# A hybrid mLSTM and S5 layer on one core: other orders in the first feed-forward round, a transfer for one weight sum, and another closing normalization

## What is computed

```python
h = rmsnorm(x, g_mix); proj = h @ w_in + b_in          # mixers A (mLSTM) and B (S5)
...
x = x + mix                                            # mix: gated outputs @ w_out
hf = rmsnorm(x, g_ffn)                                 # D_FF = 2816 = 22 tiles of 128
x = x + (silu(hf @ w_ff1) * (hf @ w_ff3)) @ w_ff2
y = rmsnorm(x, g_final)                                # returned, with the mixers' states
```

## Time and profile before

| | |
|---|---|
| median of 3 runs | 924.69 us (924.21 to 926.32) |
| the profiled execution: device time | 924.23 us |
| its span in the trace | 922.5 us |
| PE busy | 899.5 us (98% of the span) |
| DVE busy | 679.7 us (74%) |
| ACT busy | 506.6 us (55%) |
| POOL busy | 264.5 us (29%) |

### The profile page before, as it was taken

The page is one execution under the profiler, slowest core; times in us unless marked ns, Lnnn a source line. Parts: engine busy times, 40 slices in busy tenths (PEclk is TensorE's granted clock), DMA queues, the critical chain, the costliest instruction groups (busy, mean ns, idle before and its releaser), DMA issues. The chain is left out here.

```text
span 922.5 us, 20670 instructions
## 1 busy us (share of the span) xinstructions
PE 899.5 (98%) x8538; PEld 866.3 (94%) x8538; DVE 679.7 (74%) x1115; ACT 506.6 (55%) x860; POOL 264.5 (29%) x420
## 2 busy tenths in 40 slices
PE   8999999999999999999999999899999999999987
PEld 4899998999899899999999999899999999999976
DVE  6869993694596476954334479999987899877977
ACT  5469628918845974823333345666534566435542
POOL 6788876722724013000000001112211111212110
PEclk9999999999999999999999999999999999999998
DMA  7523137253336226352323536588888678888742
GB/s 304 184 81 107 68 103 265 104 223 129 106 119 229 72 80 237 102 219 95 114 92 114 139 114 136 119 215 183 181 176 185 159 183 193 196 175 172 147 90 93
DMA packets 50676, 138.44 MB, mean 150 GB/s; under 512 B 4340, under 2 KB 10020, under 8 KB 48664
## 3 DMA queue, kind: packets, MB, share of 16 engines
q1 hardware_dynamic: 31744, 79.64, 26.4%
q0 software_dynamic: 16608, 50.08, 24.2%
q10 hardware_dynamic: 2232, 7.41, 2.3%
HBM read 123.74 MB, written 13.39 MB: 149 GB/s over the span
## 5 line engine op out<-in xcount | busy, mean ns | idle before, releaser
L562 ACT ACTIVATE w_high<-raw 128x1024 fp32r<-128x1024 f32 (+1 forms) x146 | 152.2, 1047 | 171.5 <-PE G L1964 95.8
L1266 POOL DMA_DIRECT2D w_sums<-wst x34 | 48.4, 1423 | 413.5 <-DVE w_low L1769 284.8
L1304 DVE TENSOR_TENSOR w_low<-raw,w_high 128x1024 fp32r<-128x1024 f32 x78 | 98.0, 1263 | 80.5 <-ACT w_high L562 79.8
L1964 PE MATMUL G<-h_high,w_high 128*128 128x256 f32 (+1 forms) x640 | 130.9, 286 | 0.0
L1964 PE MATMUL G<-h_low,w_high 128*128 128x256 f32 (+1 forms) x640 | 129.0, 283 | 0.0
L1964 PE MATMUL G<-h_high,w_low 128*128 128x256 f32 (+1 forms) x640 | 128.9, 283 | 0.0
L1964 PEld LDWEIGHTS G<-h_high,w_high 128*128 128x128 f32 x640 | 99.2, 188 | 2.0 <-issue 1.6
L1964 PEld LDWEIGHTS G<-h_high,w_low 128*128 128x128 f32 x640 | 99.4, 188 | 0.0
L1964 PEld LDWEIGHTS G<-h_low,w_high 128*128 128x128 f32 x640 | 99.1, 188 | 0.0
L1769 DVE TENSOR_TENSOR w_low<-raw,w_high 128x1024 fp32r<-128x1024 f32 (+1 forms) x68 | 80.9, 1190 | 13.9 <-ACT w_high L562 13.7
L2286 PE MATMUL G<-ffn_in_high,w_high 128*128 128x260 f32 x308 | 87.3, 283 | 3.6 <-DVE up_a L1843 1.5
(11 more groups left out here) (455 smaller groups left out, 2422.5 us busy)
## 6 DMA issues: line engine op xcount, KB each, us to landing
raw<-wst SPq DMA_DIRECT2D x124, 512.0 KB, 3.5
w_sums<-wst POOLq DMA_DIRECT2D x30, 512.0 KB, 7.5
c_samples<-c POOLq DMA_DIRECT2D x4, 2048.0 KB, 8.8
out_cs<-c_samples POOLq DMA_DIRECT2D x4, 2048.0 KB, 7.6
w_sums<-wst SPq DMA_DIRECT2D x15, 512.0 KB, 4.5
raw<-wst POOLq DMA_DIRECT2D x15, 512.0 KB, 6.2
v_spread<-v_scratch ACTq DMA_DIRECT2D x4, 1024.0 KB, 6.3
raw<-wst SPq DMA_DIRECT2D x6, 384.0 KB, 3.2
```

Source lines behind the costliest of these rows:

```text
L562: return act.activation(out, in_, ACT.Copy, **kw)
L1266: pool.dma_start(halves_of(tile, r), block_of(r, row, col), accum_op=ALU.add).then_inc(s, 16)
L1304: tt(WL[n.slot()][:], raw[n.slot()][:], WH[n.slot()][:].bitcast(F32), ALU.subtract).then_inc(w_lo, 1)
L1964: last = mm(o, w[slot][:, c], h[:, k, c0_:c0_ + width], start=start and x == 0 and t == 0, stop=stop and x == n - 1 and t == 2)
```

## The change

`LAST` is 7, and `square_of(m)` holds the old wait and Square of chunk m. Two places are changed: the way from the last output chunk through the first up round, and the last two rounds with the end.

```diff
@@ SP @@
             for r in range(1, NR):
-                sp.wait_ge(s4_ready, r)
+                if r == 1:
+                    sp.wait_ge(s4_first, 16)
+                else:
+                    sp.wait_ge(s4_ready, r - 1)
                 load_a12(r)
...
@@ ACT @@
-                for q in ((0, 1), (2,), (3,))[m - 5] if m >= 5 else ():
+                for q in ((0, 1), (2,))[m - 5] if m in (5, 6) else ():
                     split_high(q)
+                if m < LAST:
+                    square_of(m)
+                else:
+                    act.activation(junk_a[:, 1:2], eps[:], ACT.Sqrt)
                 act.wait_ge(xg_ready, KC + m + 1)
...
+            split_high(3)
+            square_of(LAST)
@@ ACT, up_round @@
                 next_high(1)
                 next_high(2)
-                take(3, x, 0, took_x3)
                 if r == 0:
                     act.wait_ge(sq_summed, 2)
...
+                take(3, x, 0, took_x3)
                 next_high(3)
...
                 next_high(4)
+                if r == 0:
+                    act.activation(junk_a[:, 2:3], eps[:], ACT.Silu)
                 next_high(5)
@@ ACT, down_round @@
+                    if r == NR - 2 and i >= 5:
+                        for m in (0, 1) if i == 5 else (4, 5):
+                            act.wait_ge((took_z5, took_x6)[m // 4], 2 * r + m % 4 + 1)
+                            act.activation(sqf[m % 4 + m // 4 * 2][:], X1[:, m, :], ACT.Square).then_inc(sq_ready, 1)
+            def scale_by_gain(m, part):
+                copy(X1[:, m, part], X1[:, m, part], scale=g_fin[:, m:m + 1]).then_inc(gained, 1)
...
@@ POOL @@
                 sum_first(r)
+                if r == 0:
+                    pool.wait_ge(s_in[0], 32)
+                    pool.wait_ge(w_lo, N_FF + 4)
+                    pool.wait_ge(a12_in, 16)
+                    add_block(FB[0], 0, 0, 1, s4_first)
                 if r + 1 < NR:
                     sum_22(r + 1)
@@ DVE, output chunks @@
-                for q in ((0, 1), (2,), (3,))[m - 5] if m >= 5 else ():
+                for q in ((0, 1), (2,))[m - 5] if m in (5, 6) else ():
                     split_low(q)
-                if m == KC - 1:
-                    sum_12(0)
-                if m >= 1:
+                if 1 <= m < LAST:
                     add_square(m)
...
+            split_low(3)
+            add_square(LAST)
@@ DVE, down_round @@
-                        if last and i >= 5:
+                        if last and i == 6:
                             dve.wait_ge(s, 2 * r + su + 1)
-                            tt(sqh[2 * i - 6 + su][:], part, part, ALU.mult).then_inc(x2_late, 1)
+                            tt(sqh[6 + su][:], part, part, ALU.mult).then_inc(x2_late, 1)
                         if last and i == 6 and su == 0:
-                            invert(1)
+                            add_half_square(5, H1)
+                            add_half_square(6, H0)
+                    if last and i < 3:
+                        add_whole_square(i + 1)
+                    elif last and i < 5:
+                        for su in range(2):
+                            add_half_square(2 * i - 6 + su, (H0, H1)[i - 3])
+                    elif last and i == 5:
+                        add_half_square(4, H1)
                     for j in (i,) if then is None else then:
                         next_low(r, j)
...
-                    stt(part, part, g_fin[:, m:m + 1], (Q, G)[half][:, 3, 0:HALF], ALU.mult, ALU.mult).then_inc(y_dve, 1)
+                part = X1[:, m:m + 2, (H0, H1)[half]]
+                tt(part, part, (Q, G)[half][:, 3:4, 0:HALF].broadcast_to([P, 2, HALF]), ALU.mult).then_inc(y_dve, 1)
@@ PE @@
-                        elif r == NR - 1 and i == 6 and su == 1:
-                            part_product(r, i, su, ks[:1], True, False)
-                            sum_squares(1, range(3))
-                            sum_squares(0, range(1))
-                            last = part_product(r, i, su, ks[1:], False, True)
...
+            sum_squares(1, False)
+            sum_squares(0, False)
             spread_inverse(1)
-            sum_squares(0, range(1, 3))
+            sum_squares(0, True)
             spread_inverse(0)
```

More of the change, by code:

```diff
@@ L553, in _ @@
                 load_a22(r)
-            for half, m in [(half, m) for half in (1, 0) for m in range(0, KC, 2)]:
-                sp.wait_ge(y_dve, KC * (1 - half) + m + 1)
+            for count, (half, m) in enumerate(scale_order):
+                sp.wait_ge(y_dve, count + 1)
                 sp.dma_start(y_o[:, m, (H0, H1)[half]], X1[:, m, (H0, H1)[half]]).then_inc(y_out, 16)
@@ L585, in _ @@
             act.wait_ge(consts, 1)
-            act.activation(junk_a[:], eps[:], ACT.Sqrt)
+            act.activation(junk_a[:, 0:1], eps[:], ACT.Sqrt)
             act.wait_ge(w_in[0], 16)
@@ L991, in down_round, with final_part @@
+                    if r == NR - 1:
+                        final_part(r, i)
                 if r >= 2 and splits_late(r - 2):
                     hidden_high(up_index(r - 2), hid_at(r - 2))
+            def scale_by_gain(m, part):
+                copy(X1[:, m, part], X1[:, m, part], scale=g_fin[:, m:m + 1]).then_inc(gained, 1)
+            def final_part(r, i):
+                if i == 2 or i == 4:
+                    m0, part, s = (2, H0, took_y2) if i == 2 else (6, H1, took_x4)
+                    for su in range(2):
+                        act.wait_ge(s, 2 * r + su + 1)
+                        act.activation(sqh[i - 2 + su][:], X1[:, m0 + su, part], ACT.Square).then_inc(sq_ready, 1)
+                elif i == 3:
+                    act.wait_ge(sq_ready, 2 * KC + 4)
+                    for m in (0, 1, 4, 5):
+                        scale_by_gain(m, slice(0, T))
+                    act.wait_ge(sq_ready, 2 * KC + 6)
+                    for m in (2, 3):
+                        scale_by_gain(m, H0)
+                elif i == 5:
+                    for su in range(2):
+                        act.wait_ge(took_z5, 2 * r + su + 1)
+                        act.activation(sqh[4 + su][:], X1[:, 2 + su, H1], ACT.Square).then_inc(sq_ready, 1)
+                    act.wait_ge(sq_ready, 2 * KC + 8)
+                    for m in (6, 7):
+                        scale_by_gain(m, H1)
+                    act.activation(junk_a[:, 0:1], eps[:], ACT.Sqrt)
+                    act.wait_ge(sq_ready, 2 * KC + 10)
+                    for m in (2, 3):
+                        scale_by_gain(m, H1)
+                elif i == 6:
+                    for su in range(2):
+                        act.wait_ge(x2_late, su + 1)
+                        scale_by_gain(6 + su, H0)
+                        if su == 0:
+                            root_of_half(1)
@@ L994, in _, with root_of_half @@
+            def root_of_half(half):
+                act.wait_ge(sq_summed, 4 - half)
+                act.activation(rt[:, 3 * half:3 * half + 3], (Q, G)[half][:, 1, 0:3], ACT.Sqrt, bias=eps[:, 0:1], scale=1.0 / D).then_inc(root_ready, 1)
             for r, (kind, _, _) in enumerate(ROUNDS):
                 up_round(r) if kind == "up" else down_round(r)
[L996 to L998 removed]
```

119 lines of the change are left out of this document (55 added, 64 removed).

## The result

| | before | after |
|---|---|---|
| median of 6 runs each, taken together | 924.7 us (922.75 to 926.32) | 927.36 us (926.36 to 928.25) |
| ratio, with its 95% interval | 1 | 1.0032 (1.0017 to 1.0046) |
| the profiled execution: device time, span | 924.23, 922.5 us | 927.45, 925.7 us |
| PE, DVE, ACT busy | 899.5, 679.7, 506.6 us | 897.0, 677.6, 514.5 us |
| first product of round 0 to first of round 15 (the second last) | 561.68 to 872.26: 310.58 us | 561.28 to 874.46: 313.18 us |

The changed kernel is 0.3% slower, and the interval excludes no change. Of the 3.2 us between the two spans, 2.6 arise between the first product of round 0 and that of round 15. The end takes 1.0 us more, and the first product of round 0 came 0.4 earlier.

The account below looks back on a forecast made before the run. PE is busy for 98% of the span, so time is won or lost only at PE's stops and the end. 924.23 + 2.1 (first place) + 0.1 (end) = 926.4 us, range 923.4 to 928.0.

Parts of the forecast that it names:

- The stop in unit 2 goes: Round 0, last chunk's low part: PE's 1.15 us stop vanishes, about 1.3 us with the slow first matmul.
- Issue and landing: POOL's added transfer for unit 5's weights: issued at 569.85, takes 5.8 us, lands at 575.65.
- The reciprocal 1.4 later: DVE, ahead of round 1: the reciprocal starts at 579.7 in place of 578.28, +1.4 us.
- PE's stops: Round 0: PE stands 1.0 us at unit 5 and 3.2 us, not 1.5, ahead of round 1.
- The clock falls behind the stop: Behind the 3.2 us stop ahead of round 1: the clock likely falls, costing 1.7 us, partly covered by 0.95 us to spare.
- The first place +2.1: Last output chunk through first up round: +2.1 us with the clock's fall, +1.4 without.
- The last round: DVE's sums ahead of units 5 and 6's low parts delay unit 3's take; PE goes on 1.0 us later, stopping about 1.2.
- The end +0.1: Kernel's end: first scaling 0.6 us later, first output 0.85 later, denser output transfers save 0.7; together +0.1 us.
- The early landing: Rival: the added transfer lands as fast as a plain load, 3.5 us, giving 923.4; chance 0.12.
- The late one (7.3): Rival: the added transfer takes 7.3 us, everything behind it 1.5 later, giving 927.9; chance 0.18.
- The clock didn't hold: Concerns the rival that the clock holds behind the stop ahead of round 1, giving 925.7; chance 0.18.
- The end wasn't bound by DVE: Concerns the rival that DVE, not the transfers, bounds the end: 1.3 us less, giving 925.0; chance 0.12.

Follow-up runs that it names:

- The chunk's order alone: Kernel before with only the last chunk's high and low parts moved ahead; fourth sum on DVE, table loads, roots and end as before: 922.69 us, ratio 0.9987.
- the copies ahead: Changed kernel with ACT copying unit 3's product in round 0 ahead of unit 5's high part, so ahead of the wait for the transfer: 926.58 us, ratio 1.0038.
- the first place alone: Kernel before with the change from last chunk through first up round only, transfer included; last rounds and end as before: 926.87 us, ratio 1.0044.
- the sum on DVE: Changed kernel with round 0's fourth sum added by DVE, not the transfer: 921.33 us, ratio 0.9973; the same with before's end: 920.76 us, 0.9965.
- the kernel without early loads: Kernel before with the new first-up-round order, fourth sum on DVE, old end, but without the two early table loads (Sqrt, Silu): 921.57 us, ratio 0.9968.
- the end alone: Changed kernel with the first up round as before, so only the last two rounds and end changed: 924.35 us, ratio 1.0001.
- the sums behind: Changed kernel with round 0's fourth sum on DVE and, in the last round, DVE's three whole-square sums moved behind taking unit 3: 921.25 us, ratio 0.9970.
- the transfer alone: Kernel before with one edit: the first round's fourth sum made by POOL's adding transfer, not DVE; old order kept: 924.76 us, ratio 1.0003.

## Why the prediction was right, and where it wasn't

The forecast was 926.4 with a range to 928.0; 927.36 lies in it, and what came is "slower by over 0.2%", to which it gave 0.38 beside 0.52 for no change. The sum was made on the profiled execution: +2.2 there, where the two spans differ by 3.2 (2.6 for the first place, 1.0 for the end, less 0.4 for the earlier start). The mechanism (the transfer holds ACT, DVE and then PE, and the clock falls) is what the runs show. Its steps, in turn:

- **The stop in unit 2 goes: right.** The chunk's order alone brought 1.4 us (predicted 1.3).
- **Issue and landing: the issue right, the landing mis-sized.** Issued at 569.39 with a round that began 0.4 us earlier, that is at 569.8 on before's clock (predicted 569.85). It took 6.44 us, not 5.8, between the quiet row and the other. I called the stretch quiet, but another transfer of POOL, of which I knew, was under way with it. This trace has the longest of five: in the others ACT went on 5.99 to 6.25 us behind the issue, and 6.52 here, so 0.2 to 0.45 of the miss is there in all of them.
- **The reciprocal 1.4 later: right but for the landing.** It starts 18.67 us behind the first product of round 0, before 16.60: +2.07, which is the 1.4 and the 0.64 of the landing.
- **PE's stops: wrong place.** I had 1.0 us at unit 5 and 3.2 ahead of round 1. There was one of 5.22 at unit 4. The step that failed is my list of what is queued behind the wait: it named the high parts and roots and left out the copies of unit 3's product, which the change itself moved behind the roots. The order of ACT in the text ahead shows them. With the copies ahead of the wait, the trace had just the two stops of the prediction, 1.10 and 3.15.
- **The clock falls behind the stop: right, 1.8 us** (2.94 + 1.74 against 2 x 1.44), predicted 1.7, and partly covered as said: kept at 1.00 it gave back about 0.5 (0.9, of which 0.4 are a faster landing), where the sum had 0.7.
- **The first place +2.1: measured +2.6.** That the total is so near is in part luck. The landing adds 0.64 and the misplaced stop about 0.3, which makes 3.0. With the copies ahead of the wait, where PE stops just as predicted, the sum with that trace's landing (6.0) would be 2.3 and the trace has 1.9. So some 0.4 of the sum was too much, and the runs don't divide it further.
- **The last round: the stop ahead of unit 4 was 1.11** (predicted about 1.2), by the sums that DVE makes ahead of the low parts. In the five other traces with this end it is 1.6 to 1.9.
- **The end +0.1: in two traces +1.0, in medians not to be told from nothing.** Against round 15's first product (2.20 us later) the first scaling is at 914.4, predicted 914.0, and before 913.43. PE was ready as predicted (its last product of the round ends at 910.8 on before's clock, predicted 910.9; the products in question are twelve and not eighteen, but the rows' 2.6 us are theirs). The mis-sized term is ACT's gain products ahead of the root, two in 0.90 us and three in 1.30, against my 0.6 and 0.8: in-place copies with a gain of 128x260 follow each other at 0.43 us. The transfers ran at 316 to 368 GB/s from their second slice, for 6.3 us (predicted 6.35), but before took 6.75, not my 7.0. So 0.4 more at the scaling and 0.25 less saved. The first output begins at 918.2, 1.3 us later than before by this clock, where 0.85 was predicted, which is that same 0.4. About 0.2 of the 1.0 stay unexplained. The medians give for the new end -1.1 us (after against the first place alone), +0.1 (alone) and +0.7 (both with the sum on DVE, against before's end), each uncertain by more than 1 us. The prediction's +0.1 fits them all; what the true value is stays open. The last section has what the traces say when those with the same fall of the clock are compared.
- **The rivals.** The early landing is out, since even 256 KB took 4.93 us. The late one (7.3) is true in part (6.44). The clock didn't hold. The end wasn't bound by DVE, since the transfers follow each other without a gap.

What the prediction lacked most is a comparison that it never made: it weighed the change as one piece, and what is in it is a gain of 3.15 us and a loss of 5.8 (by the distances of the traces), of which the loss comes from one line.

## What to carry to other kernels

Before a short sum on a busy engine (here 1.15 us on DVE) is given to a transfer, measure from the moment at which its operand is free to the first use, not its place in the list: below the landing of such a transfer (6 us here) everything behind the wait is late, and an order that frees the operand later makes the same transfer dear (nothing in the old order, 5.8 us in the new). List every instruction behind a new wait in the **new** order, copies that free a PSUM bank before all, and ask of each what PE can't start without it. When a change bundles several edits, price the sign of each by itself: the good part may be hidden under one bad line.

## What the runs showed of the hardware

The clock's fall isn't tied to a stop of a given length. In the second last round all fourteen kernels have nearly the same stops of PE: 1.78 us, and then 0.48 and 2.22, or 1.40 where the clock had fallen. Before, after and the kernel without early loads fell to 0.50 behind the 2.22. Five fell behind the 1.78 already (the end alone, the copies ahead, the sums behind, the transfer alone, the order alone), and six didn't fall at all between 872 and 896 us. Part of what a fall takes is hidden by later waits: with the new end as it was changed, the stop ahead of unit 4 of the last round is 1.11 us where the fall came late, and 1.6 to 1.9 in the others. There are more falls behind that. In the trace of the end alone the clock fell a second time in the last round, behind the stop of 1.83 us (0.50 over 902 to 904; stops of 1.61 to 1.90 at the same place in four other traces were followed by none). Near the end it fell in most traces, at moments that differ. The rows are twelve records of small products, for the squares of the second token half, first in before, then in the kernel without the early loads:

```profile
913.01 1.48 PE L2357 MATMUL Q<-ones,x_half_squares 128*128 128x1 f32 x12
```
```profile
911.00 2.70 PE L2366 MATMUL Q<-ones,x_half_squares 128*128 128x1 f32 x12
```

The granted clock was 0.98 over 913 to 914.5 in the former and 0.50 over 911 to 913.7 in the latter. In the six traces with the old end this group took 1.48 us once, before, and 2.06 to 2.70 in the five others. So two traces can differ by a microsecond or more at the end without a cause in the code, as the column "end" of the table shows (49.3 to 52.8): its two largest values (52.6 and 52.8) belong to the two traces just named. Among the traces without a fall between 872 and 896 us, the old end took 49.5 and 50.05, the end as changed 50.8 to 51.2 (three traces). That is about 1.1 us more for the new end, in line with the 1.0 above, but from five traces, and the medians can't confirm it. In the first up round it was regular: the stops of 3.15, 3.72, 4.95 and 5.22 us were each followed by a fall, and those of 1.10 to 1.84 by none.
